# First heads of three attention stages loaded in the tail of the stage in front

## The chip, the cores and the metric

The kernel runs on one core of a Trainium2 chip. The metric is the device time of one launch in microseconds (us). The core has a matrix engine (TensorE, PE; its weight loads are PEld), a vector engine (VectorE, DVE), a scalar engine (ScalarE, ACT), a general engine (GpSimd, POOL) and a sequencer that computes nothing and issues DMAs (SyncE, SP). Each has its own instruction stream and they meet only at semaphores. All DMAs of the parts spoken of here are issued by SP, in the order of its program.

## The reference

Two blocks in sequence on 1024 tokens of width 1024, all in float32. What matters here is which attention follows which projection:

```python
# first block
proj = rms_norm(x) @ w_in                        # qa ka va za qb kb vb zb
oa = diff_attention(q1, q2, k1, k2, va, lam, t5_bias)      # 4 heads, dense
yb = neighbourhood_attention(qb, kb, vb, na_rpb) * silu(zb) # 8 heads, 8 x 16 window
x = x + concat([ya, yb]) @ w_out
x = x + sigmoid(x @ w_ple_gate) * (p @ w_ple_proj)
# second block, twice
proj = h @ w_in[l]                               # q_d k_d v_d cq ckv k_rope
o_dil = dilated_attention(q_d, k_d, v_d, pos, slopes)       # 8 heads, three dilations
o_mla = latent_attention(cq, ckv, k_rope, ...)              # 8 heads, 64 + 32 rotary columns
x = x + gt1 * (concat([o_dil, o_mla]) @ w_out[l])
x = x + gt2 * (square(relu(h @ w_mlp_in[l])) @ w_mlp_out[l])
```

## The kernel before

The program is a list of stages with a barrier between most of them: first projection (`pj1`), differential attention (`diff`), neighbourhood attention (`na`), output product, gate; then for each layer L of two the second projection (`pj2`), dilated attention (`dil`), latent attention (`mla`), output product and MLP. A barrier is `Eng.barrier`: each engine drains, signals, and waits for the four others, SP too.

Memory on chip (SBUF) is laid out by hand: each stage has its own set of tensors that start at the same address, so a tensor of one stage lies upon others of the stage before. Queries, keys and values go from the projection to the attention through DRAM scratch (`QA_d`, `KA_d`, `VA_d`, `QB_d`, `KB_d`, `QM_d`, `KM_d`, `KR_d`, `VM_d`). In `pj2` the weights come in pieces: SP loads a piece into `RAW` (3 slots), ACT rounds it into `WH`, POOL subtracts to get `WL` (line 426) and signals `w_ready`. The 64 tiles of `pj2` are done in this order: 8 latent tiles, 16 + 16 tiles in pairs, and 24 tiles in groups of three: values (`v`, 24 matmuls), then two halves of the latent keys and values (`mkv`, 3 matmuls each). DVE copies values into `VB` (2 slots: a tile's copy waits until the store of the tile two before it has landed), SP stores them (`v_store`), and ACT and DVE write `HI` and `LO` (3 slots), which SP stores as well. SP works through the tiles in `proj_sp`, one wait after another.

An attention stage has 8 heads of 8 units (64 units, 128 queries each). `heads_sp` loads a head's queries and keys into one of two slots, head h in slot h % 2, values for two heads at a time; from head 2 on a load waits for `full`, the score units of the head that had the slot. In `na` POOL adds bias and mask (`BIn`, line 1655), which DVE needs for a unit, and in `dil` POOL first regroups the queries (`QCd`, line 1665) and DVE needs the distance table `ND`: tile 0 for unit 0 (`nd0`), tiles 1 to 3 for unit 1 (`nd1`), tiles 4 to 7 for unit 4 (`nd2`). In `na` POOL also clears 16 cells of `PThn`/`PTln` before its first unit. All five stages' first heads are loaded behind the barrier:

```python
            for h in range(8):
                slot, p = h % 2, h // 2
                if h >= 2:
                    e.wait_ge(s["full"], a.u0 + 8 * (h - 1))
                ld = a.loaded(h)[0]
...
        def mla_attention(who, L):
            e, key, s = who.e, who.key, AT["mla"]
            if key == "sp":
                for slot in range(2):
                    e.dma_start(KMh[NOPE:DQ, slot, :].bitcast(F32), KR_d[0]).then_inc(s["pos"], 16)
```

## Time and profile before

| | before |
|---|---|
| median of 3 runs | 4240.02 us (4237.3 to 4242.52) |
| time of the profiled execution | 4249.0 us |
| its span, first to last instruction | 4247.2 us |
| mean granted TensorE clock | 0.96 |
| PE busy | 91% of the span |
| DVE, ACT, POOL busy | 49%, 36%, 39% |
| moved by DMA | 402.33 MB, 95 GB/s over the span |

The profiled execution's own time is 9 us above the median of the other runs, 1.8 us of it outside the span. Busy shares are means over stages with different limits; the stage starts spoken of here are short stretches in which PE does nothing, and a mean doesn't show them. TensorE runs at one of two levels of the clock, 1.2 or 2.4 GHz, given as 0.50 and 1.00 of full speed.

### The profile page before, as it was taken

Reading aid. Unit: us, or ns where it says so; the run is one execution under the profiler, and the core shown is the slowest. Engines: PE = TensorE matmul, PEld = TensorE weight load, DVE = VectorE, ACT = ScalarE, POOL = GpSimd, SP = SyncE. Lnnn points to the kernel's source line nnn. Section 1 sums busy time; section 2 is a strip of 40 time slices with the busy share of each in tenths; the row PEclk is TensorE's granted clock in tenths of the full one; section 3 lists DMA queues with packets and bytes.
Section 4 is the critical chain, followed back from the end, with each engine's and each line's share of the span. In section 5 each row is a group of like instructions: output and inputs, shape, how many; then the busy total and the mean of one; then the engine's idle time right before and its main releaser. Section 6 shows DMA issues by size and latency. Waiting matters only on the chain.

```text
span 4247.2 us, 52791 instructions
## 1 busy us (share of the span) xinstructions
PE 3845.7 (91%) x19336; PEld 3210.4 (76%) x19336; DVE 2101.1 (49%) x3607; ACT 1529.5 (36%) x2777; POOL 1650.4 (39%) x1426
## 2 busy tenths in 40 slices
PE   2899796998789798998999999889899998999999
PEld 1788675876678687877888888777778877888887
DVE  2445285832466576744445443465567733333333
ACT  1212175732233475642221221333566632222221
POOL 2524034732454450024444444453540025444442
PEclk8999898999999899999999999899899999999999
DMA  7567344631245533222223322245522121111111
GB/s 168 159 197 212 105 124 89 125 112 62 79 116 135 143 73 76 49 95 70 94 80 97 102 75 55 76 123 136 134 69 66 43 95 60 50 50 40 60 40 55
DMA packets 285833, 402.33 MB, mean 95 GB/s; under 512 B 43876, under 2 KB 206820, under 8 KB 285028
## 3 DMA queue, kind: packets, MB, share of 16 engines
q1 hardware_dynamic: 278664, 373.79, 31.6%
q10 hardware_dynamic: 6912, 25.17, 2.1%
q8 instruction: 155, 2.54, 0.3%
q14 instruction: 102, 0.84, 0.1%
HBM read 311.60 MB, written 96.45 MB: 96 GB/s over the span
## 4 chain that ended last, share of the span: by engine, by line
PE 69%; issue 10%; POOL 7%; DVE 5%; POOLq 2%; ACT 2%; SPq 2%; DMA 2%; DVEq 1%; ACTq 0%
PE ps L477 6%; PE ps L479 6%; PE ps L478 6%; PE ps L2308 5%; PE ps L2310 5%; PE ps L2309 5%; PE ps L2326 5%; PE ps L2328 5%; PE ps L2327 5%; PE ps L1766 3%; POOL WL L426 2%; POOL rs L839 2%; PE ps L1461 2%; PE ps L1451 1%; PE ps L1452 1%
## 5 line engine op out<-in xcount | busy, mean ns | idle before, releaser
L426 POOL TENSOR_TENSOR WL<-RAW,WH 128x1024 fp32r<-128x1024 f32 x226 | 554.8, 2469 | 739.5 <-ACT WH L408 729.2
L477 PE MATMUL ps<-WH,XTh 128*128 128x512 f32 (+1 forms) x1536 | 616.6, 401 | 61.0 <-POOL WL L426 35.8
L478 PE MATMUL ps<-WH,XTl 128*128 128x512 f32 (+1 forms) x1536 | 604.1, 393 | 0.0
L479 PE MATMUL ps<-WL,XTh 128*128 128x512 f32 (+1 forms) x1536 | 604.0, 393 | 0.0
L408 ACT ACTIVATE WH<-RAW 128x1024 fp32r<-128x1024 f32 x226 | 233.7, 1057 | 800.8 <-PE ps L2328 362.7
L2348 DVE TENSOR_TENSOR X<-ps,X 128x512 f32<-128x512 f32 x512 | 349.2, 689 | 258.5 <-PE ps L2328 257.5
L2326 PE MATMUL ps<-WH,Hh 128*128 128x512 f32 x1024 | 403.1, 394 | 16.1 <-issue 11.7
L2308 PE MATMUL ps<-XTh,WH 128*128 128x512 f32 x1024 | 401.3, 392 | 14.9 <-issue 11.6
L2309 PE MATMUL ps<-XTl,WH 128*128 128x512 f32 x1024 | 399.8, 390 | 0.0
L2327 PE MATMUL ps<-WH,Hl 128*128 128x512 f32 x1024 | 399.8, 390 | 0.0
L2328 PE MATMUL ps<-WL,Hh 128*128 128x512 f32 x1024 | 399.8, 390 | 0.0
L2310 PE MATMUL ps<-XTh,WL 128*128 128x512 f32 x1024 | 399.8, 390 | 0.0
L2339 DVE TENSOR_TENSOR MT<-ps,MT 128x512 f32<-128x512 f32 x128 | 88.5, 692 | 625.6 <-ACT MT L2362 625.6
L477 PEld LDWEIGHTS ps<-WH,XTh 128*128 128x128 f32 x1536 | 296.1, 193 | 126.2 <-issue 61.1
L479 PEld LDWEIGHTS ps<-WL,XTh 128*128 128x128 f32 x1536 | 295.1, 192 | 58.8
L478 PEld LDWEIGHTS ps<-WH,XTl 128*128 128x128 f32 x1536 | 295.9, 193 | 53.9
L2377 POOL TENSOR_TENSOR Hl<-MT,Hh 128x512 fp32r<-128x512 f32 x128 | 165.6, 1294 | 438.7 <-ACT Hh L2366 438.7
L2326 PEld LDWEIGHTS ps<-WH,Hh 128*128 128x128 f32 x1024 | 193.1, 189 | 64.9 <-DVE X L2348 13.0
L2308 PEld LDWEIGHTS ps<-XTh,WH 128*128 128x128 f32 x1024 | 193.2, 189 | 55.9 <-issue 16.1
L2362 ACT ACTIVATE MT<-ps 128x512 f32<-128x512 f32 x128 | 76.4, 597 | 433.8 <-PE ps L2310 428.5
L2328 PEld LDWEIGHTS ps<-WL,Hh 128*128 128x128 f32 x1024 | 193.1, 189 | 40.7
L2310 PEld LDWEIGHTS ps<-XTh,WL 128*128 128x128 f32 x1024 | 193.1, 189 | 40.5
(257 smaller groups left out, 7823.3 us busy)
## 6 DMA issues: line engine op xcount, KB each, us to landing
...
X_d<-X SPq DMA_DIRECT2D x2, 4096.0 KB, 12.0
...
```

The lines of the kernel that those rows point to most:

```text
L408: e.activation(w_high(n), w_raw(n), ACT.Copy).then_inc(w_rounded, 1)
L426: e.tensor_tensor(w_low(n), w_raw(n), w_high(n).bitcast(F32), ALU.subtract).then_inc(w_ready, 1)
L477: e.matmul(bank, a, w, start=(kc == 0), stop=False)
L478: e.matmul(bank, b, w, start=False, stop=False)
L479: j = e.matmul(bank, a, l, start=False, stop=(kc == K - 1))
L2308: e.matmul(bank, w, xh, start=(kc == 0), stop=False)
L2309: e.matmul(bank, w, xl, start=False, stop=False)
L2310: j = e.matmul(bank, l, xh, start=False, stop=(kc == KC - 1))
L2326: e.matmul(bank, Hh[:, half, et, tq], w, start=(et == 0), stop=False)
L2327: e.matmul(bank, Hl[:, half, et, tq], w, start=False, stop=False)
L2328: j = e.matmul(bank, Hh[:, half, et, tq], l, start=False, stop=(et == 1))
L2348: e.tensor_tensor(X[:, t, cs], ps[:, 4 + (step * 16 + k) % (3 if mod else 4), :], X[:, t, cs], ALU.add).then_inc(s["yt"], 1)
```

## The change

The first head's loads of `na`, `dil` (both layers) and `mla` (both layers) move ahead of the barrier, into SP's program of the stage in front. Their places in SBUF are moved so that slot 0 of the next stage lies upon memory that the running stage no longer uses: for `na` upon the differential stage's slot 0, for `mla` upon the dilated stage's slot 0, and for `dil` upon `RAW`, the raw weights of `pj2`.

- `diff`: when three of four heads are finished (`used`), SP issues the mask `RMK`, head 0's queries, keys and bias table `NAB`, and the values and gates of `na`.
- `pj2`: at step nt - 14 = 50 of 64, SP waits until the last weight piece is split (`w_ready`) and all key tiles are stored, then issues the five loads of queries and keys of dilated head 0. Values and `ND` stay behind the barrier; `ND` tile 0 is now the first DMA there.
- `dil`: behind its last head's loads SP waits for unit 56 of `full` and the sixth `vlo`, then issues the rotary keys, queries, keys and values of latent head 0.
- The rotary keys of slot 1 are loaded with latent head 1, behind the barrier, and the semaphore `pos` of `mla` is dropped.
- POOL's clears in `na` move from in front of its first unit to in front of `value_low` at unit 3; in `dil` its wait for the step table `LM` moves behind the first regrouping.

The program has as many DMAs as before. The core of the diff:

```diff
         c2 = ExitStack()
-        PTnh, PTnl, VSn, VHLn, OTn = head_tiles(c2, "n", 6)
         QSn, KHn, KLn = sb("QSn", [P, 2, S], F32R, c2), sb("KHn", [P, 2, S], F32R, c2), sb("KLn", [P, 2, S], F32R, c2)
-        ZSn = sb("ZSn", [P, 2, T, P], c=c2)
+        PTnh = sb("PTnh", [P, 2, 6, 512], F32R, c2)
+        VSn, ZSn = sb("VSn", [P, 2, T, P], c=c2), sb("ZSn", [P, 2, T, P], c=c2)
+        PTnl = sb("PTnl", [P, 2, 6, 512], F32R, c2)
+        VHLn, OTn = sb("VHLn", [P, 2, T, P], F32R, c2), sb("OTn", [P, 2, 512], c=c2)
         Pn, BIn = sb("Pn", [P, 3, NA_KEYS], c=c2), sb("BIn", [P, 3, NA_KEYS], c=c2)
+        TMPn = sb("TMPn", [P, 256], c=c2)
+        sb("diff_rest", [P, 896], c=c2)
         NAB = sb("NAB", [P, 2, NA_E * GRID_W], c=c2)
         RMK = sb("RMK", [P, 3, NA_KEYS], c=c2)
-        TMPn = sb("TMPn", [P, 256], c=c2)
         c2.close()
 
...
-        PTdh, PTdl, VSd, VHLd, OTd = head_tiles(c2, "d", 6)
-        QSd, KHd, KLd = sb("QSd", [P, 2, S], F32R, c2), sb("KHd", [P, 2, S], F32R, c2), sb("KLd", [P, 2, S], F32R, c2)
-        QCd = sb("QCd", [P, 2, T, P], F32R, c2)
+        PTdh, PTdl = sb("PTdh", [P, 2, 6, 512], F32R, c2), sb("PTdl", [P, 2, 6, 512], F32R, c2)
+        VSd, QCd = sb("VSd", [P, 2, T, P], c=c2), sb("QCd", [P, 2, T, P], F32R, c2)
+        QKd = sb("QKd", [P, 2, 3, S], F32R, c2)
+        QSd, KHd, KLd = QKd[:, :, 0, :], QKd[:, :, 1, :], QKd[:, :, 2, :]
+        VHLd, OTd = sb("VHLd", [P, 2, T, P], F32R, c2), sb("OTd", [P, 2, 512], c=c2)
...
-        PTmh, PTml, VSm, VHLm, OTm = head_tiles(c2, "m", T)
-        QMh, QMl = sb("QMh", [DQ, 2, S], F32R, c2), sb("QMl", [DQ, 2, S], F32R, c2)
-        KMh, KMl = sb("KMh", [DQ, 2, S], F32R, c2), sb("KMl", [DQ, 2, S], F32R, c2)
-        Pm = sb("Pm", [P, 2, S], c=c2)
+        PTmh = sb("PTmh", [P, 2, T, 512], F32R, c2)
+        Pm, VHLm = sb("Pm", [P, 2, S], c=c2), sb("VHLm", [P, 2, T, P], F32R, c2)
+        VSm, KMl = sb("VSm", [P, 2, T, P], c=c2), sb("KMl", [DQ, 2, S], F32R, c2)
+        QKm = sb("QKm", [DQ, 2, 3, S], F32R, c2)
+        QMh, QMl, KMh = QKm[:, :, 0, :], QKm[:, :, 1, :], QKm[:, :, 2, :]
+        OTm, PTml = sb("OTm", [P, 2, 512], c=c2), sb("PTml", [P, 2, T, 512], F32R, c2)
...
                 for piece in pj.plan.loads(n):
                     w_load(e, piece)
+                if pj.s is PJ["pj2"] and n == pj.nt - 14:
+                    e.wait_ge(w_ready, FIRST_PIECES + L * LAYER_PIECES + N_IN2)
+                    last_key = max(m for k, m in pj.tr.items() if pj.tiles[k][0] == 3)
+                    for i in range(ST_SLOTS):
+                        e.wait_ge(stored(s, i), L * 64 * uses(pj.ntr, i) + 64 * uses(last_key + 1, i))
+                    head_loads(e, Heads("dil", L, 1 + 2 * L), 0)
                 if pj.mod and n - MOD_LAG - 12 in (2 * KC, 5 * KC):
...
                     load_v(e, ZA_d, h, slot, ZS, ld)
+                e.wait_ge(s["used"], a.c(0) + H_DIFF - 1)
+                following = Heads("na", 0, 0)
+                e.dma_start(RMK[:].rearrange("p a b -> p (a b)"), A["near_mask"]).then_inc(following.s["pos"], 16)
+                e.wait_ge(PRE["bst"], 16 * H_NA)
+                head_loads(e, following, 0)
+                value_loads(e, following, 0)
...
-                return (self.s["ld0"], self.s["ld1"])[h % 2], 16 * self.loads * (4 * self.run + h // 2 + 1)
+                rope = 2 * (self.run + 1) if self.kind == "mla" else 0
+                return (self.s["ld0"], self.s["ld1"])[h % 2], 16 * (self.loads * (4 * self.run + h // 2 + 1) + rope)
...
                 if u == 3:
+                    for t2 in range(T):
+                        n, n0, r = len(na_tiles(t2)), na_tiles(t2)[0] - 2 * (t2 // 4), t2 % 4
+                        for k in [k for k in range(6) if not n0 <= k < n0 + n]:
+                            e.memset(PTnh[:, t2 // 4, k, r * P:r * P + P].bitcast(F32), 0.0)
+                            e.memset(PTnl[:, t2 // 4, k, r * P:r * P + P].bitcast(F32), 0.0)
                     value_low(e, a, 0)
...
             queries(0)
+            e.wait_ge(s["pos"], a.run * 16 + 64)
...
+        def head_loads(e, a, h):
+            s, slot = a.s, h % 2
+            ld = a.loaded(h)[0]
+            if a.kind == "mla":
+                if h < 2:
+                    e.dma_start(KMh[NOPE:DQ, slot, :].bitcast(F32), KR_d[0]).then_inc(ld, 16)
+                    e.dma_start(KMl[NOPE:DQ, slot, :].bitcast(F32), KR_d[1]).then_inc(ld, 16)
+                e.dma_start(QMh[:, slot, :].bitcast(F32), QM_d[h, 0]).then_inc(ld, 16)
+                e.dma_start(QMl[:, slot, :].bitcast(F32), QM_d[h, 1]).then_inc(ld, 16)
+                e.dma_start(KMh[0:NOPE, slot, :].bitcast(F32), KM_d[h, 0]).then_inc(ld, 16)
+                e.dma_start(KMl[0:NOPE, slot, :].bitcast(F32), KM_d[h, 1]).then_inc(ld, 16)
+            if a.kind == "dil":
+                load64(e, QA_d, KA_d, h, slot, QSd, KHd, KLd, ld)
+            if a.kind == "na":
+                load64(e, QB_d, KB_d, h, slot, QSn, KHn, KLn, ld)
+                if h >= 2:
+                    e.wait_ge(s["bias"], a.own + 8 * (h - 1))
+                for a2 in range(2):
+                    e.dma_start(NAB[64 * a2:64 * a2 + 64, slot, :].rearrange("p (a b) -> p a b", b=GRID_W),
+                                NAB_d[h][:, 1 - a2:1 - a2 + NA_E, GRID_W - 1:2 * GRID_W - 1]).then_inc(ld, 16)
+        def value_loads(e, a, p):
+            s = a.s
+            vld = a.v_loaded(p)[0]
+            if p >= 2:
+                e.wait_ge(s["vlo"], a.h0 + 2 * p - 2)
+            load_v(e, {"na": VB_d, "dil": VA_d, "mla": VM_d}[a.kind], p, p % 2, a.VS, vld)
+            if a.kind == "dil":
+                v = VA_d.rearrange("t p c -> (t p) c")[:, p * P:p * P + P]
+                e.dma_start(VFS[:, p % 2, 0:4, :], v[S - 448:S].rearrange("(b r) c -> b r c", r=4)).then_inc(vld, 16)
+                e.dma_start(VFS[:, p % 2, 4:8, :], v[0:448].rearrange("(b r) c -> b r c", r=4)).then_inc(vld, 16)
+            if a.kind == "na":
+                if p >= 2:
+                    e.wait_ge(s["out"], a.g0 + 4 * p - 4)
+                load_v(e, ZB_d, p, p % 2, ZSn, vld)
+
         def heads_sp(who, a):
             e, s = who.e, a.s
+            if a.kind == "dil":
+                e.dma_start(ND[:, 0, :], ND_d[0]).then_inc(s["nd0"], 16)
+                e.dma_start(LM[:], A["logstep"]).then_inc(s["pos"], 16)
             for h in range(8):
                 if h >= 2:
                     e.wait_ge(s["full"], a.u0 + 8 * (h - 1))
+                if h >= 1:
+                    head_loads(e, a, h)
+                if h % 2 == 0 and (h >= 1 or a.kind == "dil"):
+                    value_loads(e, a, h // 2)
                 if a.kind == "dil" and h < 2:
                     for t in range(ND_FIRST[h + 1], ND_FIRST[h + 2]):
                         e.dma_start(ND[:, t, :], ND_d[t]).then_inc((s["nd1"], s["nd2"])[h], 16)
+            if a.kind == "dil":
+                e.wait_ge(s["full"], a.u0 + 56)
+                e.wait_ge(s["vlo"], a.h0 + 6)
+                following = Heads("mla", a.run, 2 + 2 * a.run)
+                head_loads(e, following, 0)
+                value_loads(e, following, 0)
 
         def heads_pe(who, a):
...
         def dil_attention(who, L):
-            e, key, s = who.e, who.key, AT["dil"]
-            if key == "sp":
-                e.dma_start(LM[:], A["logstep"]).then_inc(s["pos"], 16)
-            if key == "pool":
-                e.wait_ge(s["pos"], L * 16 + 64)
             band_heads(who, Heads("dil", L, 1 + 2 * L))
 
         def mla_attention(who, L):
-            e, key, s = who.e, who.key, AT["mla"]
-            if key == "sp":
-                for slot in range(2):
-                    e.dma_start(KMh[NOPE:DQ, slot, :].bitcast(F32), KR_d[0]).then_inc(s["pos"], 16)
-                    e.dma_start(KMl[NOPE:DQ, slot, :].bitcast(F32), KR_d[1]).then_inc(s["pos"], 16)
-            if key == "pe":
-                e.wait_ge(s["pos"], L * 64 + 64)
             heads(who, Heads("mla", L, 2 + 2 * L))
 
```

What stands on SP in the tail of `pj2` of layer 0, before the change: the stores of latent keys (`KM_d`), of latent values (`VM_d`) and of dilated values (`VA_d`), group after group.

```order
L2242 DMA KM_d<-LO 64x4x128
L2246 DMA VM_d<-VB 128x256 x2
L901 DMA VA_d<-VB 128x512
L2242 DMA KM_d<-HI 64x4x128
L2242 DMA KM_d<-LO 64x4x128
L2242 DMA KM_d<-HI 64x4x128
```

And with the change: five loads stand between the stores of one group and those of the next (`QKd` holds `QSd`, `KHd` and `KLd` side by side).

```order
L2259 DMA KM_d<-LO 64x4x128
L2263 DMA VM_d<-VB 128x256 x2
L948 DMA QKd<-QA_d 128x1024
L950 DMA QKd<-KA_d 64x1024
L951 DMA QKd<-KA_d 64x1024
L950 DMA QKd<-KA_d 64x1024
L951 DMA QKd<-KA_d 64x1024
L909 DMA VA_d<-VB 128x512
```

So every store behind that place, five tiles of dilated values, ten half tiles of latent values and twelve of latent keys, is now issued behind five loads.

What SP issues behind the barrier for dilated attention of layer 0, before the change, up to head 1's first load:

```order
L1951 DMA LM<-logstep 128x384
L940 DMA QSd<-QA_d 128x1024
L942 DMA KHd<-KA_d 64x1024
L943 DMA KLd<-KA_d 64x1024
L942 DMA KHd<-KA_d 64x1024
L943 DMA KLd<-KA_d 64x1024
L1727 DMA ND<-ND_d 128x688
L947 DMA VSd<-VA_d 128x8x128
L1735 DMA VFS<-VA_d 112x4x128
L1736 DMA VFS<-VA_d 112x4x128
L1743 DMA ND<-ND_d 128x688 x3
L940 DMA QSd<-QA_d 128x1024
```

And with the change:

```order
L1764 DMA ND<-ND_d 128x688
L1765 DMA LM<-logstep 128x384
L955 DMA VSd<-VA_d 128x8x128
L1754 DMA VFS<-VA_d 112x4x128
L1755 DMA VFS<-VA_d 112x4x128
L1775 DMA ND<-ND_d 128x688 x3
L948 DMA QKd<-QA_d 128x1024
```

The five loads of queries and keys are gone from the front of this list, and `ND` tile 0 leads it; the rest keeps its order.

What POOL does first in neighbourhood attention (from the last two clears on), before the change, with the semaphores waited for:

```order
L1900 MEMSET PThn 128x128
L1901 MEMSET PTln 128x128
L1655 TENSOR_TENSOR BIn<-NAB,RMK 128x640 [waits na_ld0,na_pos]
L1655 TENSOR_TENSOR BIn<-NAB,RMK 128x640 x2
L1640 TENSOR_TENSOR VHLn<-VSn,VHLn 128x8x64 [waits heads_vhi]
L1655 TENSOR_TENSOR BIn<-NAB,RMK 128x640 [waits heads_max] x5
```

And with the change, from its first instruction behind the barrier on:

```order
L1675 TENSOR_TENSOR BIn<-NAB,RMK 128x640 [waits stage_done_sp,stage_done_act,stage_done_dve,stage_done_pe,na_ld0,na_pos]
L1675 TENSOR_TENSOR BIn<-NAB,RMK 128x640 x2
L1667 MEMSET PTnh 128x128
L1668 MEMSET PTnl 128x128
L1667 MEMSET PTnh 128x128
```

The first bias sum (line 1675 now) has no clear in front of it any more, and all sixteen clears stand between the third sum and the low half of the values.

## Rows read from the trace of the kernel before

**Rows 1.** Page, part 1: busy us, share of the span, instructions.

```profile
PE 3845.7 (91%) x19336; PEld 3210.4 (76%) x19336; DVE 2101.1 (49%) x3607; ACT 1529.5 (36%) x2777; POOL 1650.4 (39%) x1426
```

**Rows 2.** Timeline, neighbourhood start: start, us, engine, line, operation [idle before <-releaser].

```profile
694.59 0.35 SPq L1895 DMA_DIRECT2D RMK<-near_mask  x1
...
696.77 0.20 POOL L1901 MEMSET PTln<- 128x128 f32 x1
...
710.11 0.79 PE L1451 MATMUL ps<-KHn,QSn 128*128 128x512 f32 x1 [19.04 <-DMA NAB<-NAB_d]
710.21 4.55 POOL L1655 TENSOR_TENSOR BIn<-NAB,RMK 128x640 f32<-128x640 f32 x3 [13.23 <-DMA NAB<-NAB_d]
...
718.55 1.28 POOL L1640 TENSOR_TENSOR VHLn<-VSn,VHLn 128x512 fp32r<-128x512 f32 x1 [3.78 <-ACTq L1550]
```

**Rows 3.** Timeline, dilated start, layer 0; last row: the same unit 4 in layer 1.

```profile
1404.03 0.34 SPq L1951 DMA_DIRECT2D LM<-logstep  x1
...
1414.72 2.12 POOL L1665 CAST QCd<-QSd 128x512 fp32r<-128x512 f32 x2 [17.94 <-DMA KLd<-KA_d]
...
1423.40 0.87 DVE L1583 CUSTOM_DVE_ANT_0 Pd<-ps,ND 128x688 f32<-128x688 f32 x1 [4.61 <-DMA ND<-ND_d]
...
1434.75 0.88 DVE L1583 CUSTOM_DVE_ANT_0 Pd<-ps,ND 128x688 f32<-128x688 f32 x1 [4.63 <-PE ps L1452]
...
3006.06 0.87 DVE L1583 CUSTOM_DVE_ANT_0 Pd<-ps,ND 128x688 f32<-128x688 f32 x1 [3.98 <-issue]
```

**Rows 4.** Windows: stretch, length, PE, PEld, DVE, ACT, POOL busy, clock, DMA share, GB/s.

```profile
1361.00:1368.00 7.00, 7.00 (x35) 5.67 (x34) 4.34 (x9) 2.30 (x4) 2.38 (x4) 1.00 0.55 150
1403.80:1434.80 31.00, 15.30 (x58) 13.11 (x58) 5.62 (x13) 7.27 (x16) 10.39 (x14) 0.52 0.90 231
1463.00:1469.00 6.00, 6.00 (x43) 5.20 (x42) 5.19 (x12) 4.54 (x11) 4.56 (x5) 1.00 0.99 251
2973.80:3007.00 33.20, 14.44 (x58) 12.37 (x58) 6.46 (x14) 7.27 (x16) 10.39 (x14) 0.55 0.87 216
```

**Rows 5.** Timeline, latent starts of both layers, and the last dilated load.

```profile
1549.47 0.60 SPq L943 DMA_DIRECT2D KLd<-KA_d  x1
...
1603.91 0.34 SPq L1960 DMA_DIRECT2D KMh<-KR_d  x1
...
1613.85 0.77 PE L1756 MATMUL ps<-KMh,QMh 96*128 96x512 f32 x1 [10.94 <-DMA KMl<-KM_d]
...
3177.13 0.34 SPq L1960 DMA_DIRECT2D KMh<-KR_d  x1
...
3188.10 0.77 PE L1756 MATMUL ps<-KMh,QMh 96*128 96x512 f32 x1 [11.97 <-DMA KMl<-KM_d]
```

**Rows 6.** Chain that ended last, in order of time: the last differential head begins.

```profile
653.38 2.33 POOL ZS L1335
```

**Rows 7.** Windows around the latent start of layer 0, same columns as rows 4.

```profile
1602.00:1604.00 2.00, 0.91 (x8) 0.77 (x7) 0.60 (x2) 0.00 (x0) 0.00 (x0) 1.00 0.02 4
...
1616.00:1618.00 2.00, 2.00 (x6) 1.52 (x6) 1.22 (x1) 0.29 (x1) 1.27 (x1) 0.53 1.03 270
```

**Rows 8.** Timeline, tail of the second projection, layer 0.

```profile
1331.92 2.40 POOL L426 TENSOR_TENSOR WL<-RAW,WH 128x1024 fp32r<-128x1024 f32 x1
...
1358.89 1.65 SPq L2246 DMA_DIRECT2D VM_d<-VB  x2
...
1362.31 0.32 SPq L901 DMA_DIRECT2D VA_d<-VB  x1
...
1365.97 1.57 SPq L2246 DMA_DIRECT2D VM_d<-VB  x2
...
1366.63 0.41 DVE L779 COPY VB<-ps 128x256 f32<-128x256 f32 x1
...
1368.72 0.69 DVE L803 COPY VB<-ps 128x512 f32<-128x512 f32 x1 [1.68 <-DMA VM_d<-VB]
...
1369.11 0.60 PE L683 MATMUL ps<-ident,QN 128*64 128x128 f32 x4
```

More of the change, by code:

```diff
@@ L254, in build_program @@
         c2.close()
-        def head_tiles(c, n, keys):
-            return [sb("PTh" + n, [P, 2, keys, 512], F32R, c), sb("PTl" + n, [P, 2, keys, 512], F32R, c),
-                    sb("VS" + n, [P, 2, T, P], c=c), sb("VHL" + n, [P, 2, T, P], F32R, c), sb("OT" + n, [P, 2, 512], c=c)]
         c2 = ExitStack()
@@ L344, in build_program @@
         AT = {"diff": {**diff_loop, **sems("diff", "map0 map1 rest")}, "na": {**heads_all, **sems("na", loads + " bias")},
-              "dil": {**heads_all, **sems("dil", loads + " bias qc nd0 nd1 nd2")}, "mla": {**heads_all, **sems("mla", loads)}}
+              "dil": {**heads_all, **sems("dil", loads + " bias qc nd0 nd1 nd2")}, "mla": {**heads_all, **sems("mla", "ld0 ld1 vld0 vld1")}}
         out_names = sems("out", "full upd")
@@ L1705, in heads_sp @@
         def heads_sp(who, a):
             e, s = who.e, a.s
+            if a.kind == "dil":
+                e.dma_start(ND[:, 0, :], ND_d[0]).then_inc(s["nd0"], 16)
+                e.dma_start(LM[:], A["logstep"]).then_inc(s["pos"], 16)
             for h in range(8):
-                slot, p = h % 2, h // 2
                 if h >= 2:
                     e.wait_ge(s["full"], a.u0 + 8 * (h - 1))
-                ld = a.loaded(h)[0]
-                if a.kind == "mla":
-                    e.dma_start(QMh[:, slot, :].bitcast(F32), QM_d[h, 0]).then_inc(ld, 16)
-                    e.dma_start(QMl[:, slot, :].bitcast(F32), QM_d[h, 1]).then_inc(ld, 16)
-                    e.dma_start(KMh[0:NOPE, slot, :].bitcast(F32), KM_d[h, 0]).then_inc(ld, 16)
-                    e.dma_start(KMl[0:NOPE, slot, :].bitcast(F32), KM_d[h, 1]).then_inc(ld, 16)
@@ L1717, in heads_sp @@
-                if a.kind == "dil":
-                    load64(e, QA_d, KA_d, h, slot, QSd, KHd, KLd, ld)
-                if a.kind == "na":
-                    load64(e, QB_d, KB_d, h, slot, QSn, KHn, KLn, ld)
-                    if h >= 2:
-                        e.wait_ge(s["bias"], a.own + 8 * (h - 1))
-                    for a2 in range(2):
-                        e.dma_start(NAB[64 * a2:64 * a2 + 64, slot, :].rearrange("p (a b) -> p a b", b=GRID_W),
-                                    NAB_d[h][:, 1 - a2:1 - a2 + NA_E, GRID_W - 1:2 * GRID_W - 1]).then_inc(ld, 16)
@@ L1726, in heads_sp @@
-                if a.kind == "dil" and h == 0:
-                    e.dma_start(ND[:, 0, :], ND_d[0]).then_inc(s["nd0"], 16)
-                if h % 2 == 0:
-                    vld = a.v_loaded(p)[0]
-                    if p >= 2:
-                        e.wait_ge(s["vlo"], a.h0 + 2 * p - 2)
-                    load_v(e, {"na": VB_d, "dil": VA_d, "mla": VM_d}[a.kind], p, p % 2, a.VS, vld)
-                    if a.kind == "dil":
-                        v = VA_d.rearrange("t p c -> (t p) c")[:, p * P:p * P + P]
-                        e.dma_start(VFS[:, p % 2, 0:4, :], v[S - 448:S].rearrange("(b r) c -> b r c", r=4)).then_inc(vld, 16)
-                        e.dma_start(VFS[:, p % 2, 4:8, :], v[0:448].rearrange("(b r) c -> b r c", r=4)).then_inc(vld, 16)
-                    if a.kind == "na":
-                        if p >= 2:
-                            e.wait_ge(s["out"], a.g0 + 4 * p - 4)
-                        load_v(e, ZB_d, p, p % 2, ZSn, vld)
+                if h >= 1:
+                    head_loads(e, a, h)
@@ L1892, in na_attention @@
             e, key, s = who.e, who.key, AT["na"]
-            if key == "sp":
-                e.wait_ge(PRE["bst"], 16 * H_NA)
-                e.dma_start(RMK[:].rearrange("p a b -> p (a b)"), A["near_mask"]).then_inc(s["pos"], 16)
             if key == "pool":
-                for t in range(T):
-                    n, n0, r = len(na_tiles(t)), na_tiles(t)[0] - 2 * (t // 4), t % 4
-                    for k in [k for k in range(6) if not n0 <= k < n0 + n]:
-                        e.memset(PTnh[:, t // 4, k, r * P:r * P + P].bitcast(F32), 0.0)
-                        e.memset(PTnl[:, t // 4, k, r * P:r * P + P].bitcast(F32), 0.0)
-                e.drain()
                 e.wait_ge(s["pos"], 16)
```

1 line of the change is left out of this document (removed).

## The prediction

> **What bounds the kernel now.** I read the page first: PE is busy for 91% of the span [rows 1], so most of the time is matmuls that this change leaves alone. It can only pay in the stretches where PE does nothing. So I went through the timeline at every barrier behind which a head is loaded. There are five, and all look alike: SP issues the first load right behind the barrier, and PE's first matmul names a DMA as what ended its wait.
>
> At the neighbourhood start SP issues at 694.59, PE begins at 710.11 and POOL's first bias sum at 710.21, all released by the bias table's landing [rows 2]. At the two latent starts it is 1603.91 to 1613.85 and 3177.13 to 3188.10 [rows 5].
>
> The dilated start is another case. POOL regroups the queries at 1414.72, 10.7 us behind the first issue, but the next wait is no shorter: DVE takes unit 1 at 1423.40, when tiles 1 to 3 of the distance table are there, and unit 4 at 1434.75 [rows 3]. The trace puts the second wait down to PE, whose matmuls for that unit were long done; what comes then is the table's tiles 4 to 7. The windows show why: from 1403.8 to 1434.8 the DMA engines are 0.90 busy at 231 GB/s, in layer 1 0.87 at 216 GB/s [rows 4]. There the queue of bytes is the bound, not one load.
>
> **Neighbourhood start: 15.5 us.** Mask, queries, keys, bias table and values are now in place at the barrier, so POOL's first sum can begin where SP's first issue stood: 710.11 - 694.59 = 15.5. The loads themselves run under the last differential head, which begins at 653.38 [rows 6], 41 us ahead of the barrier; they are 4.2 MB by their shapes, 19 us even at 216 GB/s, and that head's own data were issued before them. The sixteen clears cost 2.4 us (the last ends at 696.97, behind the barrier of 694.6). They used to be hidden under the load; now they stand between POOL's third sum and the values, where POOL idles 3.78 us for ACT [rows 2]. So they stay hidden, with 1.4 us to spare, and I cost them at nothing (2.4 us if that cover were gone). Late next could be head 1, issued at the barrier and needed at unit 8, some 21 us on (POOL's eight sums of 1.5 us and its two waits); its 2.2 MB take 10 us at 216 GB/s, and the 4.2 MB of head 0 landed 15.5 us behind their first issue. I take nothing for it.
>
> **Latent starts: 9.9 and 11.0 us, and some clock.** The loads follow the last dilated load, at 1549.47 [rows 5], once unit 56 is reached. The stage has 200 us (1404.03 to 1603.91) for eight heads, so unit 56 comes some 25 us ahead of the barrier at the latest, and the 2.1 MB, 10 us at 216 GB/s, land before it. Their queue is empty then. The first terms are 1613.85 - 1603.91 = 9.9 and 3188.10 - 3177.13 = 11.0. Besides, the clock is at the upper level until 1604 and at the lower one (0.53) still in 1616 to 1618, after 11 us without a matmul [rows 7]; with a gap of about 1 us instead it may stay up. From 1613.85 to 1618 everything PE does would take half as long, at most 2.1 us; layer 1 does the same work and gets the same figure. DVE and ACT share that stretch, so I take 1.5 us each, and keep 0 and 2.1 for the range. Sums: 11.4 and 12.5.
>
> **Dilated starts: 6.2 and 6.5 us.** Here the five loads of queries and keys leave a full queue. They are 1.57 MB (one of 128 x 1024 and four of 64 x 1024 floats). The same load for a later head of this stage, keeps all DMA engines busy for 6.0 us (0.99 from 1463 to 1469) [rows 4]. At the stage's mean rates it is 1.57/231 = 6.8 us and in layer 1 1.57/216 = 7.3. All that is issued behind it, both waits for the table included, moves by that much. I take 6.2 and 6.5, near the direct measurement, with 5.8 (at 270 GB/s [rows 7]) and 7.3 as bounds. That POOL and PE begin 10 us earlier buys nothing, since unit 1 waits for the table. The table's tile 0 is issued first now, so unit 0 is in time.
>
> **What the tail of the projection pays: 1 us per layer.** SP reaches step 50 at about 1360.5, when it has issued the pair of 1358.89, and waits there for nothing: the last weight piece is split at 1334.3 [rows 8], and the last keys were stored before that step. The five issues take SP 3.0 us, at about 0.6 each, of which 1.8 was idle before the store of 1362.31; queued behind them are the stores, and behind those DVE, which may refill a value slot only when its store has landed. A store lands 2.7 us after issue (1365.97, DVE released at 1368.72 [rows 8]), so DVE already waits there. The head load puts up to 6 us of queue in front, while the tail itself fills 0.55 of the DMA engines [rows 4]. The store of 1362.31 would go out at 1363.6 and land by about 1369; the copy that needs its slot, at 1366.63, ends at 1369.4, and PE wants its tile at 1369.11: 0.3 us late. The next copy (1368.72) becomes 2 to 3 us late, which DVE, busy 4.34 of 7 us [rows 4], makes up over the next groups. PE needs that tile's bank only four tiles on. I take 1.0, between 0 and 5.
>
> **The sum.** 15.5 + 11.4 + 12.5 + 6.2 + 6.5 - 2.0 = 50.1 us. The profiled execution took 4249.0, so the changed one would be 4198.9. It lies 9.0 above the median of the runs, 4240.0, to which the same sum is applied: 4189.9, say 4190.
>
> **Rivals.**
> *The projection's tail pays it all back (0.13).* The stores behind 1.57 MB of loads come 6 us late, and PE stops for it, since DVE's copy has no slack today (it waits 1.68 us for a store at 1368.72 [rows 8]). Both dilated terms fall to zero: 15.5 + 11.4 + 12.5 = 39.4, time 4200.6. Against it speak PE's own margins just worked out.
> The page "DMA: Bandwidth & Descriptors" of the Trainium skill (Queues, rings and completion order) says that a DMA engine takes descriptors in ring order and that a completion count lands only behind every earlier write of that engine. By that rule the first store can't report before the loads are written, about 1367 to 1369, which is what the two cases above differ over: the lateness is sure, PE's stop is not.
> *The next head is late (0.04).* Head 1 is issued at the barrier as before, but needed 10 to 15 us sooner. If it lacked 5 us at the neighbourhood and latent starts each, 15 us go: 4205. For it speaks only that the bias table's DMAs are slow; against it the margins above, 5 us and more.
> *Slower than before (0.02).* SP is blocked at step 50 by its new waits, and with it all stores of the tail. It would have to hold PE for more than (50 + 8.5)/2 = 29 us per layer to end beyond 0.2%; with the stage's whole rest of 35 us lost twice the time is 4260. The last split lies 26 us ahead of that step, which is why I give it so little.
> *More than forecast (0.04):* clock at its upper bounds and 7 us per dilated start with a tail that pays nothing, 55 us: 4185 and below.
>
> **How the numbers follow.** The forecast has 0.77. Its own range is 4185 to 4198. The range for the time is 4180 to 4206: the low end is the upper bounds of all terms (15.5 + 12.0 + 13.1 + 6.8 + 7.3 = 54.7, 4185) and 5 us for what an earlier start may give in the dilated stage; the high end takes the lower bounds with 5 us lost per tail (15.5 + 9.9 + 11.0 + 1.6 = 38.0, 4202) and the late head partly. A measurement of this kernel can tell about 0.2%, 8.5 us, from no change. Every case but the blocked SP is beyond that: faster 0.97, within 0.2% 0.01, slower 0.02.
>
> **What the changed profile would show.** Right: the first neighbourhood, latent and (POOL's) dilated instruction within 1 us of the barrier; DVE's unit 1 and unit 4 in the dilated stage about 13 and 25 us behind the barrier instead of 19.4 and 30.7; POOL's clears inside its wait for ACT; DVE's waits for value stores longer in the tail, with PE's period there unchanged. Wrong: a gap on PE of some us behind step 50, a DMA wait at unit 8 of a stage, or the clock at 0.50 through the latent starts as before. The forecast fails most easily in the tail, and if the queue's bytes are not what bounds the dilated start.

## The result and the profile after

| | before | after |
|---|---|---|
| median | 4241.27 us (4237.3 to 4250.71, 4 runs) | 4201.82 us (4198.02 to 4205.07, 4 runs) |
| ratio | | 0.9903, 95% interval 0.9885 to 0.9922 |
| time and span of the profiled execution | 4249.0, 4247.2 us | 4202.3, 4200.5 us |
| mean granted clock | 0.96 | 0.965 |

The change makes the kernel faster by 1%: 39.5 us by the medians, 41 by the ratio. The forecast of 4190.0 was 11.8 us too low. The result lies inside the range of 4180 to 4206, outside the 4185 to 4198 that I gave the likeliest case, and within 1.2 us of a rival's time (4200.6, the tail pays it all back). The two profiled executions differ by 46.7 us, 7 more than the medians. The experiments have to say which case it is and where those 7 us belong.

Page of the kernel after, part 1, to be read beside [rows 1]:

```profile
PE 3845.1 (92%) x19336; PEld 3209.2 (76%) x19336; DVE 2103.9 (50%) x3607; ACT 1531.0 (36%) x2777; POOL 1650.5 (39%) x1426
```

PE's busy time has not moved (3845.7 before). All that changed is idle time.

Timeline of the neighbourhood start after the change, beside [rows 2]:

```profile
695.30 0.33 SPq L948 DMA_DIRECT2D QSn<-QB_d  x1
695.34 0.76 PE L1466 MATMUL ps<-KHn,QSn 128*128 128x512 f32 x1 [3.56 <-DVEq L372]
695.39 4.56 POOL L1675 TENSOR_TENSOR BIn<-NAB,RMK 128x640 f32<-128x640 f32 x3 [0.88 <-DVEq L372]
...
699.88 0.21 POOL L1667 MEMSET PTnh<- 128x128 f32 x1
...
702.08 0.21 POOL L1668 MEMSET PTnl<- 128x128 f32 x1
703.72 1.27 POOL L1655 TENSOR_TENSOR VHLn<-VSn,VHLn 128x512 fp32r<-128x512 f32 x1 [1.43 <-ACTq L1565]
```

The reader is to see that PE and POOL now name another engine's barrier signal and no DMA, and begin 0.04 and 0.09 us behind SP. The clears stand in POOL's wait for ACT, of which 1.43 us are left: the cover that I counted on, with the spare that I gave it.

Timeline of the latent start in layer 0, and windows behind it (length, busy PE, PEld, DVE, ACT, POOL, granted clock, DMA share, GB/s), beside [rows 5, 7]:

```profile
1585.47 0.32 SPq L1731 DMA_DIRECT2D QKm<-KR_d  x1
...
1585.68 0.77 PE L1794 MATMUL ps<-QKm 96*128 96x512 f32 x1 [1.21 <-DVEq L372]
```

```profile
1582.00:1584.00 2.00, 1.07 (x11) 0.96 (x9) 0.60 (x2) 0.21 (x1) 0.00 (x0) 1.00 0.01 4
1584.00:1586.00 2.00, 0.79 (x6) 0.68 (x5) 0.60 (x2) 0.43 (x1) 0.00 (x0) 0.91 0.00 0
1586.00:1588.00 2.00, 2.00 (x6) 1.52 (x6) 0.00 (x0) 0.20 (x1) 1.28 (x1) 0.50 0.66 172
1588.00:1590.00 2.00, 2.00 (x6) 1.60 (x5) 1.22 (x1) 0.12 (x1) 0.00 (x0) 0.50 0.87 238
1590.00:1592.00 2.00, 2.00 (x7) 1.20 (x6) 0.82 (x1) 1.08 (x2) 0.00 (x0) 0.50 1.00 252
1592.00:1594.00 2.00, 2.00 (x12) 1.64 (x10) 1.43 (x3) 1.66 (x3) 0.00 (x0) 0.88 0.68 133
```

PE starts 0.2 us behind the barrier and idled only 1.21 us, but the clock falls all the same, and PE then runs for 6.8 us at the lower level. The clock's share of my forecast did not come.

Timeline of the dilated start (layer 0; last row, unit 4 of layer 1), and the windows from the barrier to unit 4 in both layers, beside [rows 3, 4]:

```profile
1394.28 0.33 SPq L1764 DMA_DIRECT2D ND<-ND_d  x1
1394.36 2.11 POOL L1685 CAST QCd<-QKd 128x512 fp32r<-128x512 f32 x2 [7.55 <-SPq L372]
...
1398.10 0.88 DVE L1598 CUSTOM_DVE_ANT_0 Pd<-ps,ND 128x688 f32<-128x688 f32 x1 [7.76 <-DMA ND<-ND_d]
...
1405.40 0.88 DVE L1598 CUSTOM_DVE_ANT_0 Pd<-ps,ND 128x688 f32<-128x688 f32 x1 [6.42 <-DMA ND<-ND_d]
...
1416.38 0.88 DVE L1598 CUSTOM_DVE_ANT_0 Pd<-ps,ND 128x688 f32<-128x688 f32 x1 [4.25 <-issue]
...
2972.15 0.88 DVE L1598 CUSTOM_DVE_ANT_0 Pd<-ps,ND 128x688 f32<-128x688 f32 x1 [5.24 <-issue]
```

```profile
1394.30:1416.40 22.10, 13.42 (x58) 11.48 (x58) 5.60 (x13) 7.27 (x16) 10.18 (x14) 0.61 0.93 253
2947.20:2972.20 25.00, 14.23 (x58) 12.14 (x58) 5.63 (x13) 7.27 (x16) 10.40 (x14) 0.57 0.89 223
```

POOL starts at once, and units 1 and 4 still wait for the table, 11.1 and 22.1 us behind the barrier in layer 0 (unit 4 at 25.0 in layer 1). I had said about 13 and 25. "Issue" at unit 4 is again the wait for tiles 4 to 7: the last of them lands at 22.0 us, 0.1 ahead of the unit.

Tail of `pj2`, layer 0, timeline and then DVE's waits from 1350 to 1395 (total, times, longest), beside [rows 8]:

```profile
1346.79 1.65 SPq L2263 DMA_DIRECT2D VM_d<-VB  x2
1348.61 0.32 SPq L948 DMA_DIRECT2D QKd<-QA_d  x1
...
1350.78 0.60 SPq L951 DMA_DIRECT2D QKd<-KA_d  x1
1351.42 0.58 SPq L909 DMA_DIRECT2D VA_d<-VB  x1
...
1355.45 4.08 SPq L2263 DMA_DIRECT2D VM_d<-VB  x2
...
1358.61 0.42 DVE L781 COPY VB<-ps 128x256 f32<-128x256 f32 x1 [4.00 <-DMA VA_d<-VB]
...
1359.13 0.63 PE L685 MATMUL ps<-ident,QN 128*64 128x128 f32 x4 [1.59 <-DVEq L785]
```

```profile
DVE VB L805 <- DMA VM_d<-VB: 5.7, 4, 1.5
...
DVE VB L781 <- DMA VA_d<-VB: 4.0, 1, 4.0
```

The store behind the five loads is issued at 1351.42 and releases DVE at 1358.61, 7.2 us later; the ones that I read before took 2.7. The page "DMA: Bandwidth & Descriptors" of the Trainium skill (Queues, rings and completion order) has a completion count land behind the earlier writes; by that rule the store waits for the loads' bytes, and this trace agrees with its 7.2 us. What I had not seen coming is that DVE stands for 4.0 us at one copy and PE for 1.59. The row of 4.08 us for two stores is no slow issue: the two take 0.60 and 0.33 us, and between them SP waits for the copy at 1358.61, which has to fill `VB` first.

### The profile page after: what moved, and what is told of

It reads as the page before. It is cut to its first block, busy times and chain, and to the rows that moved or that the text cites. A ratio compares the mean times of both kernels' runs of the same rounds, so it can differ in the third digit from the quotient of the medians.

```text
span 4200.5 us, 52796 instructions
## 1 busy us (share of the span) xinstructions
PE 3845.1 (92%) x19336; PEld 3209.2 (76%) x19336; DVE 2103.9 (50%) x3607; ACT 1531.0 (36%) x2777; POOL 1650.5 (39%) x1426
## 4 chain that ended last, share of the span: by engine, by line
PE 70%; issue 11%; POOL 7%; DVE 5%; POOLq 2%; ACT 2%; SPq 1%; DMA 1%; DVEq 1%; ACTq 0%
PE ps L479 6%; PE ps L480 6%; PE ps L481 6%; PE ps L2325 5%; PE ps L2327 5%; PE ps L2326 5%; PE ps L2343 5%; PE ps L2345 5%; PE ps L2344 5%; PE ps L1804 3%; POOL rs L841 2%; POOL WL L428 2%; PE ps L1476 2%; PE ps L1466 1%; PE ps L1467 1%
## 5 line engine op out<-in xcount | busy, mean ns | idle before, releaser
L479 PE MATMUL ps<-WH,XTh 128*128 128x512 f32 (+1 forms) x1536 | 617.6, 402 | 61.1 <-POOL WL L428 35.5
L2325 PE MATMUL ps<-XTh,WH 128*128 128x512 f32 x1024 | 401.4, 392 | 14.9 <-issue 11.6
L2327 PEld LDWEIGHTS ps<-XTh,WL 128*128 128x128 f32 x1024 | 193.1, 189 | 40.7
```

Source lines behind the costliest of these rows:

```text
L479: e.matmul(bank, a, w, start=(kc == 0), stop=False)
L2325: e.matmul(bank, w, xh, start=(kc == 0), stop=False)
L2327: j = e.matmul(bank, l, xh, start=False, stop=(kc == KC - 1))
```

## Experiments

Twelve kernels ran in three groups, each group on a chip of its own and beside the kernel before: `e1_all` to `e4_spread`, `e5_nd_first` to `e8_before_again`, and `e9_na_only` to `e12_no_dil_ndv`. The medians of before were 4244.04 (17 runs), 4243.06 (7) and 4238.4 us (11). A difference "by the medians" is within a group unless it says otherwise; across groups it can be off by the 5 us by which before itself moved, so there the difference of the ratios stands beside it.

**The parts.** `e1_all` is the changed kernel again.

> The changed kernel once more, on the same chip as the three that follow, as their base. Its two profiled executions with the one of before differ by 46.7 us, the medians of four unprofiled runs by 39.5. My theory (15.5 from the neighbourhood start, 6.7 and 6.1 net from the two dilated starts, 9.2 and 12.3 from the latent ones, as the two traces show) asks for about 47 us below the kernel before; the rival, that the projection's tail pays both dilated terms back, for 37 to 40. 40 or less again would mean that something that the profiled executions do not show is lost.

Measured: 4203.02 us (4198.7 to 4204.61), ratio 0.9906 (0.9891 to 0.992): 41.0 below before. The 47 us that the two single traces gave are not there.

`e2_no_dil` puts the dilated head back behind the barrier:

```diff
-                if pj.s is PJ["pj2"] and n == pj.nt - 14:
-                    e.wait_ge(w_ready, FIRST_PIECES + L * LAYER_PIECES + N_IN2)
...
-                    head_loads(e, Heads("dil", L, 1 + 2 * L), 0)
...
             if a.kind == "dil":
-                e.dma_start(ND[:, 0, :], ND_d[0]).then_inc(s["nd0"], 16)
                 e.dma_start(LM[:], A["logstep"]).then_inc(s["pos"], 16)
+                head_loads(e, a, 0)
+                e.dma_start(ND[:, 0, :], ND_d[0]).then_inc(s["nd0"], 16)
```

> The dilated head's five loads of queries and keys go back behind the barrier, with the table's tile 0 behind them, as in the kernel before; the neighbourhood and latent parts stay. My theory: the tail of the projection gets back 2.2 and 2.0 us, the dilated start loses 8.4 and 8.1, so the time is 12.3 us above the whole change (10 to 15), and DVE does not wait for a store of VA_d in the tail. Rival (the tail pays it all back): within 3 us of the whole change.

Measured: 4209.65 us (4203.34 to 4210.71), ratio 0.9922 (0.991 to 0.9934). It is 6.6 above the whole change: neither my 12.3 nor the rival's 3 or less. DVE does not wait for `VA_d` in the tail any more. Its timeline has the surprise:

```profile
1405.93 0.88 DVE L1592 CUSTOM_DVE_ANT_0 Pd<-ps,ND 128x688 f32<-128x688 f32 x1 [3.19 <-DMA ND<-ND_d]
...
1415.77 0.88 DVE L1592 CUSTOM_DVE_ANT_0 Pd<-ps,ND 128x688 f32<-128x688 f32 x1 [3.12 <-issue]
```

Its barrier is at 1389.20, so unit 4 comes 26.6 us behind it, with the order of loads that took 30.7 in [rows 3]. In layer 1 of the same trace it takes 31.9 us, as long as before, so the short time is no property of this kernel.

`e3_dil_only` has the dilated move alone; the mask, heads and values of `na` and `mla` are issued at the top of `heads_sp` again:

```diff
-                e.wait_ge(s["used"], a.c(0) + H_DIFF - 1)
...
-                head_loads(e, following, 0)
-                value_loads(e, following, 0)
```

> Only the dilated move is made; the neighbourhood and latent heads are loaded behind their barriers again. My theory: 12 to 13 us faster than before (0.3%), with 11.1 and 22.1 us from the barrier to units 1 and 4 as in the whole change. Rival (paid back): within 3 us of before. A third possibility is that the parts do not add up: then this run and the one without the dilated move together give clearly more or less than the whole change.

Measured: 4236.15 us (4231.12 to 4245.96, 12 runs), ratio 0.9986 (0.9977 to 0.9995): 7.9 us by the medians, 2 to 10 by the interval. The move pays, which rules out "all paid back", and it pays less than the 12 to 13 us that I expected here and the 10.7 of the forecast. 34.4 from `e2_no_dil` and 7.9 give 42.3, so the parts add up. DVE's wait in the tail is there as in the whole change:

```profile
DVE VB L781 <- DMA VA_d<-VB: 3.7, 1, 3.7
```

`e9_na_only` and `e10_mla_only` are the other two parts alone, by the same kind of edit.

> Only the neighbourhood move is made; latent and dilated heads are loaded behind their barriers. Every trace so far shows 15.5 us won at that start, so I expect 14 to 17 us below the kernel before in the medians. Rival: it is 12 or less, because head 1 or something else behind the start takes some back that the single traces hide.

Measured: 4225.85 us (4215.01 to 4226.86), ratio 0.9967 (0.9954 to 0.9979): 12.6 by the medians, 14.0 by the ratio. The trace has PE and POOL at the barrier as after. The measure cannot separate 12 from 15.5 here; all nine traces with this move can (below).

> Only the two latent moves are made. The traces show 8.3 to 10.2 us in layer 0 and 10.5 to 12.3 in layer 1 against the one profiled execution of before, and that one's layer 1 start was 1.7 us longer than in a second profile. My theory: 18 to 20 us below before. Rival, my forecast: 23.9 (11.4 + 12.5), with the clock's share.

Measured: 4221.36 us (4216.9 to 4224.25), ratio 0.9961 (0.9948 to 0.9973): 17.0 by the medians, 11.4 to 22.0 by the interval. My 18 to 20 is inside, my forecast of 23.9 outside.

**Was the profile of before a fair sample?** `e8_before_again` is the kernel before with no edit.

> The kernel before, profiled a second time. Its first profiled execution took 4249.0 us, 5 above the median of 17 runs, and its dilated start in layer 0 (30.7 us from the barrier to unit 4) was 4 us longer than in the run that also loads this head behind the barrier (26.6). If that was chance, this one shows 27 to 28 us there and a total near 4244; if the old order of instructions itself costs it, 30 to 31 again.

Measured: 4236.89 us, span 4235.1, 12.1 less than the first profile. Windows from the barrier to unit 4, both layers, of `e8_before_again`:

```profile
1405.50:1432.70 27.20, 13.23 (x58) 11.04 (x58) 5.57 (x12) 7.27 (x16) 8.92 (x13) 0.58 0.95 264
2972.10:2998.00 25.90, 14.50 (x57) 12.87 (x58) 5.57 (x12) 7.27 (x16) 8.85 (x13) 0.50 0.97 276
```

The very same transfers in the same order took 27.2 and 25.9 us where [rows 3] has 30.7 and 32.1, at 264 and 276 GB/s. Before had 233 and 223 GB/s from barrier to unit 4; the 216 of [rows 4] is for a window 1 us longer. So the long starts were a draw of that execution, in both layers, and larger than I had asked. `e9_na_only`, whose dilated start is in the old order too, shows the short times again:

```profile
1384.40:1410.30 25.90, 14.55 (x57) 12.92 (x58) 5.58 (x12) 7.27 (x16) 8.91 (x13) 0.50 0.97 276
2950.90:2976.20 25.30, 14.40 (x57) 12.78 (x57) 5.57 (x12) 7.28 (x16) 8.75 (x13) 0.50 0.98 282
```

**The tail.** `e4_spread` issues the five loads one by one:

```diff
-                if pj.s is PJ["pj2"] and n == pj.nt - 14:
+                if pj.s is PJ["pj2"] and pj.nt - 14 <= n < pj.nt and (n - pj.nt + 14) % 3 == 0:
+                    k = (n - pj.nt + 14) // 3
...
+                    if k == 0:
+                        e.dma_start(QSd[:, 0, :].bitcast(F32), ...)
+                    else:
+                        r, part = divmod(k - 1, 2)
+                        e.dma_start((KHd, KLd)[part][64 * r:64 * r + 64, 0, :].bitcast(F32), KA_d[0, part])...
```

> The five loads of the dilated head are issued one at a time, one behind each group of three tiles from step 50 to step 62, instead of five in a row at step 50. The bytes are the same. My theory: DVE's wait of 4.0 us for the store of VA_d falls below 1 us and PE's gap in the tail goes, so the time is about 4 us below the whole change (2.2 + 2.0), while units 1 and 4 of the dilated stage stay at 11 and 22 us behind the barrier. Rival: the last loads now lie close to the barrier, are still under way when the table's tiles are issued, and what the tail gets back the start loses: no change beyond 1 us.

Measured: 4201.02 us (4192.49 to 4204.19), ratio 0.9901 (0.9888 to 0.9914), 2.0 below `e1_all`, which this measure does not tell from nothing. In the trace DVE's wait for `VA_d` is gone, and from 1345 to 1393 its wait for the latent values is short:

```profile
DVE VB L805 <- DMA VM_d<-VB: 3.2, 2, 1.7
```

Units 1 and 4 come 13.5 and 24.2 us behind the barrier in layer 0 (11.1 and 22.1 to 22.8 with five in a row). The tail gets its time back (from 50 us ahead of the barrier on it is as long as before, in both layers) and the start gives some of it up, so neither theory holds alone.

**The queue of bytes.** `e5_nd_first` takes head 1's loads out from in front of tiles 4 to 7:

```diff
-                if a.kind == "dil" and h < 2:
-                    for t in range(ND_FIRST[h + 1], ND_FIRST[h + 2]):
-                        e.dma_start(ND[:, t, :], ND_d[t]).then_inc((s["nd1"], s["nd2"])[h], 16)
+                if a.kind == "dil" and h == 0:
+                    for t in range(1, 8):
+                        e.dma_start(ND[:, t, :], ND_d[t]).then_inc((s["nd1"], s["nd2"])[t >= ND_FIRST[2]], 16)
```

> The whole change, and tiles 4 to 7 of the distance table are issued right behind tiles 1 to 3, ahead of head 1's queries and keys (1.57 MB). My theory (behind the barrier it is the queue of bytes that unit 4 waits for): unit 4 stood 22.1 to 22.8 us behind the barrier in layer 0 and about 25 in layer 1; it now comes about 17 and 19 behind it, unit 1 stays, head 1 is in time at unit 8, and the time is 6 to 10 us below the whole change. Rival (DVE and PE set unit 4, not the table): no change. Second rival: head 1 becomes late and a wait for it at unit 8 takes back most of the gain.

Measured: 4188.72 us (4187.77 to 4191.65), ratio 0.987 (0.9853 to 0.9886), 14.3 below `e1_all` (another group; 15 by the ratios), more than my 6 to 10. DVE's units 1 to 4 in layer 0, barrier at 1393.38:

```profile
1405.83 0.87 DVE L1598 CUSTOM_DVE_ANT_0 Pd<-ps,ND 128x688 f32<-128x688 f32 x1 [7.83 <-DMA ND<-ND_d]
...
1410.52 0.88 DVE L1598 CUSTOM_DVE_ANT_0 Pd<-ps,ND 128x688 f32<-128x688 f32 x1 [1.25 <-PE ps L1467]
1412.47 0.86 DVE L1598 CUSTOM_DVE_ANT_0 Pd<-ps,ND 128x688 f32<-128x688 f32 x1
```

Unit 4 follows unit 3 without any wait (19.1 and 18.9 us behind the barriers), and the last of tiles 4 to 7 lands 2.7 and 1.4 us ahead of it. The table was the bound, and is not any more for this unit. No wait for head 1's loads shows at PE or DVE, so the second rival did not occur.

`e6_ndv` also issues tiles 1 to 3 ahead of the values:

```diff
                 e.dma_start(LM[:], A["logstep"]).then_inc(s["pos"], 16)
+                for t in range(1, ND_FIRST[2]):
+                    e.dma_start(ND[:, t, :], ND_d[t]).then_inc(s["nd1"], 16)
...
+                if a.kind == "dil" and h == 0:
+                    for t in range(ND_FIRST[2], 8):
+                        e.dma_start(ND[:, t, :], ND_d[t]).then_inc(s["nd2"], 16)
```

> As the run before, and tiles 1 to 3 of the table are also issued ahead of head 0's values (0.97 MB), tiles 4 to 7 behind the values. By the queue of bytes unit 1 comes 3 to 4 us sooner (7 to 8 us behind the barrier in place of 11 to 12.9), and unit 4 at about 16. The values are later by 4 us; if POOL, ACT or PE then wait for them, units 2 and 3 give it back. Theory: 1 to 3 us per layer below the run before; rival: the same time as it.

Measured: 4182.67 us (4181.34 to 4184.91), ratio 0.9857 (0.9842 to 0.9871), 6.0 below `e5_nd_first`. Barrier at 1389.82:

```profile
1398.08 0.87 DVE L1598 CUSTOM_DVE_ANT_0 Pd<-ps,ND 128x688 f32<-128x688 f32 x1 [2.97 <-DMA ND<-ND_d]
...
1406.71 0.87 DVE L1598 CUSTOM_DVE_ANT_0 Pd<-ps,ND 128x688 f32<-128x688 f32 x1 [1.44 <-PE ps L1467]
```

Unit 1 is 8.3 us behind the barrier in place of 12.4, unit 4 at 16.9. The row names PE for unit 4, but PE's matmuls for it end at 1405.75 and the last of tiles 4 to 7 lands at 1406.59, 0.12 us ahead of the unit. So unit 4 is back at the table's landing, 2.2 us sooner than in `e5_nd_first`; layer 1 shows the same (landing at 15.0, unit at 15.2).

> The same order behind the barrier together with the five loads spread over the tail of the projection. The spread alone took DVE's wait in the tail away but gave only 2 us by the medians. If its gain was lost at the table's queue, it should now show: 3 to 5 us below the run before. If the spread loads simply gain nothing beyond 1 us per layer, it is within 2 us of it.

`e7_spread_ndv` is both edits. Measured: 4181.49 us (4175.99 to 4182.9), ratio 0.9851 (0.9836 to 0.9866). It is within 2 us of `e6_ndv`, so spreading the loads is worth nothing that can be measured here. It has the lowest median of all, 61.6 us below before, with `e6_ndv` level with it; both beat the changed kernel by 20 us (another group; 21 to 23 by the ratios).

`e11_order_only` is the kernel before with the order of `e6_ndv` and no move; `e12_no_dil_ndv` is `e2_no_dil` with that order.

> The kernel before with none of the moves; only the distance table's tiles 1 to 3 are issued ahead of head 0's values and tiles 4 to 7 behind them, ahead of head 1. Bytes in front of unit 1 fall from 4.1 to 3.1 MB, in front of unit 4 from 7.0 to 5.5 MB. By the queue of bytes: unit 1 at 12 to 16 us behind the barrier (16.2 to 21.5 in profiles of the old order), unit 4 at 21 to 25 (25.9 to 32.1), and 10 to 16 us below before in all. Rival (the order pays only once the head load is out of the way): within 4 us of before.

Measured: 4225.48 us (4224.54 to 4227.46), ratio 0.997 (0.9959 to 0.9981): 12.9 below before. Units 1 and 4 stand at 14.9 and 22.5 us in layer 0, 16.0 and 24.0 in layer 1, as expected. The table does not bound them any more: its tiles land 1.2 to 2.0 us ahead of each, and at unit 1 it is PE that DVE waits for:

```profile
1417.20 0.87 DVE L1583 CUSTOM_DVE_ANT_0 Pd<-ps,ND 128x688 f32<-128x688 f32 x1 [0.82 <-PE ps L1452]
```

> The neighbourhood and latent moves and the new order of the table, but the dilated head behind the barrier. Against the same kernel with the dilated head in the projection's tail (4182.7 us) it tells what that move is worth when the table's order is right. Theory: 1.57 MB less queue per layer, 6 us, minus 1.7 us that the tail pays: 8 to 10 us above that kernel, 4191 to 4193. Rival: the move was only worth something because the order was bad; within 3 us of it.

Measured: 4190.53 us (4187.63 to 4192.84), ratio 0.9889 (0.9874 to 0.9905), 7.9 above `e6_ndv` (4182.67, another group; 13.6 by the ratios). The dilated move is worth at least as much with the right order as with the old one (6.6). The traces say more: over the stretches of the next section the two dilated starts gain 13 us by the move with the new order (two traces of each placement), against 8 with the old, both before the tails are paid.

## Why the forecast was right in kind and too large

With the fourteen traces of this study the terms can be measured as means. Each stretch below is taken between the same instructions of DVE (or of SP at the barrier) in every trace: from one at the end of the stage in front to one behind the start, where all traces run in step again. Other end points shift a difference of means by up to 0.3 us. The dilated rows count only traces with the table's order of the changed kernel, and the tails leave out the two with spread loads.

| term | forecast | one profile of each | stretch, old placement | stretch, new placement | difference |
|---|---|---|---|---|---|
| neighbourhood start | 15.5 | 15.5 | 40.3 (39.9 to 40.9, 5 traces) | 24.45 (24.43 to 24.46, 9) | 15.9 |
| latent start, layer 0 | 11.4 | 9.2 | 60.2 (59.4 to 61.2, 5) | 50.3 (49.2 to 51.2, 9) | 10.0 |
| latent start, layer 1 | 12.5 | 12.3 | 36.0 (35.5 to 37.5, 5) | 26.2 (25.0 to 26.9, 9) | 9.8 |
| dilated start, layer 0 | 6.2 | 8.7 | 93.2 (90.2 to 96.3, 5) | 88.0 (87.6 to 88.3, 3) | 5.2 |
| dilated start, layer 1 | 6.5 | 7.9 | 121.6 (117.0 to 126.2, 5) | 118.6 (118.3 to 119.1, 3) | 3.0 |
| tail, layer 0 | -1.0 | -2.4 | 47.1 (46.8 to 47.5, 7) | 48.7 (48.2 to 49.2, 5) | -1.6 |
| tail, layer 1 | -1.0 | -1.6 | 53.8 (53.7 to 54.0, 7) | 55.4 (55.2 to 55.6, 5) | -1.6 |
| sum | 50.1 | 49.6 | | | 40.7 |

The means give 40.7 us; the medians 39.5 and 41.0. Point by point:

- *Neighbourhood start*: right, in place, size and cover. Head 1 was not late: the nine new stretches agree within 0.03 us.
- *Latent starts*: the first term of layer 0 (9.9) was right, that of layer 1 (11.0) 1.2 too large, and the 1.5 us of clock in each did not come. The step that failed is "with a gap of about 1 us instead it may stay up". PE idled 1.21 us and the clock was low for 6.8 us after the change; in `e6_ndv`, at the same place, for 3.4:

```profile
1574.00:1576.00 2.00, 1.16 (x4) 1.01 (x5) 0.35 (x1) 0.63 (x1) 0.56 (x1) 0.85 0.11 47
1576.00:1578.00 2.00, 2.00 (x6) 1.52 (x6) 0.73 (x1) 0.00 (x0) 0.71 (x1) 0.50 0.84 277
1578.00:1580.00 2.00, 1.63 (x7) 1.00 (x6) 1.04 (x2) 1.21 (x2) 0.00 (x0) 0.79 1.07 277
1580.00:1582.00 2.00, 2.00 (x14) 1.67 (x12) 1.50 (x3) 1.46 (x3) 0.00 (x0) 1.00 0.99 172
```

  In most of the starts the gap is not what took the clock down. The clock fell in all eighteen latent starts with the new placement, and in ten of them it had fallen 0.9 to 2.2 us before the gap of 1.21 us began. `e1_all`, layer 1, where the gap ends at 3143.65:

```profile
3139.00:3140.00 1.00, 0.57 (x6) 0.43 (x4) 0.32 (x2) 0.31 (x1) 0.00 (x0) 1.00 0.00 0
3140.30:3142.30 2.00, 1.80 (x8) 1.78 (x8) 0.00 (x0) 0.00 (x0) 0.00 (x0) 0.50 0.00 0
3142.30:3143.60 1.30, 0.14 (x1) 0.00 (x0) 0.60 (x2) 0.06 (x1) 0.00 (x0) 0.50 0.00 0
```

  It rose again 3.7 to 9.4 us behind PE's first matmul (5.6 on average), against 3.9 to 9.6 (6.1) in the ten starts with the old placement. So the matmuls behind the barrier run at the lower level about as long as before, and the clock gives next to nothing back. Layer 1's 11.0 was read from the longest of five starts (37.5; the others 35.5 to 35.8), 1.5 above their mean.
- *Dilated starts*: the mechanism is shown. The queue of bytes in front of the table is the bound: unit 4 moves with the bytes ahead of it (27.6 and 28.6 us on average with 7.1 MB up to tile 7, 22.5 and 24.4 with 5.6 MB), and order alone, with not a byte less in all, gives 12.9 us. The terms 6.2 and 6.5 were too large by 1.0 and 3.5. What failed is that the bytes left would move at an unchanged rate. At the mean rates of the old order, 259 and 250 GB/s, 1.57 MB are 6.1 and 6.3 us, near what I took (estimates, bytes over mean time to unit 4). But the 5.6 MB left moved at 248 and 228 GB/s, so unit 4 came only 5.1 and 4.2 us sooner, and in layer 1 another 1 us went behind it. With three traces of the new placement the two differences are uncertain by some 1 and 2 us (the scatter of the five old ones, 2.3 and 4.4, over the root of five); their sum less the two tails, 5.0 us, agrees with the 6.6 and 7.9 of the medians, so part of the shortfall may be the draw.
- *The tail*: 1.6 us per layer and not 1.0, within my 0 to 5. In layer 0 the copy was late by 4 us, not by 2 to 3, and PE stood for 1.59 us where I had it 0.3 late. In layer 1 the loss is as large, but its trace shows no single wait for `VA_d`; there the cause is not shown.
- *The rival* whose time fits (4200.6) is refuted: with the dilated move alone the kernel is faster by 2 to 10 us, and without it the whole change is 6.6 us slower. The late head and a blocked SP did not occur.

The terms together are 9.4 us too large: 4.5 in the dilated starts, 4.1 in the latent ones, 1.2 in the tails, and 0.4 the other way at the neighbourhood start. The rest of the 11.8 is small: the median of before is 1.3 us above the one that I used, and means and medians differ by about as much.

One profile is a risky source for such terms. That of before lies 9.0 us above the median, and all of it inside the span, since the 1.8 us between time and span are in every run (4202.3 and 4200.5 after). Against the means above it is 3.1 and 4.7 us long at the dilated starts and 1.5 at the second latent start, 0.8 and 0.3 short at the first latent and the neighbourhood start, about 8 in sum. That is most of why the two profiles show 46.7 us and the medians 40. Into my forecast it went by the second latent term alone, since I took the dilated terms from bytes and rates.

The table leaves one thing out. Its one-profile column sums to 49.6, 3 us above the 46.7, because a stretch that no edit touches, between the same two DVE instructions inside `na` and ahead of the tail of the first `pj2` (793.0 to 1340.9 us before, 778.2 to 1329.1 after), is 3.1 us longer after the change. Of the seven traces with the dilated loads in the tail, five have it at 550.5 to 550.9 us and one each at 549.7 and 547.5; the seven without have 547.7 to 548.8. That is 2.1 us more on average with the move. Whether it belongs to the move, and by what, is open; with it the means give 38.6 us.

What stays open: why the same queue of transfers drains at 223 in one execution and at 282 GB/s in the next. In the old order the three starts above 30 us show DMA shares of 0.90 and 0.91, the seven below 28 us 0.93 to 0.98, so the DMA engines had more gaps in the former. That is the smaller part: rate over share, my estimate of what they moved while busy, is 248 to 256 GB/s in the long starts and 276 to 288 in the short ones. No run here tells what makes either. Nor was it tried what would keep the clock up across the latent barrier.
